# A two-layer hybrid encoder (pooling, RWKV-7, SwiGLU): where ScalarE scales the running state in chunks 4 to 7 of each head pair

## The reference, cut to what matters

```python
kk = heads(k * k_k)
kk = kk / jnp.maximum(jnp.sqrt(jnp.sum(kk * kk, axis=-1, keepdims=True)), 1e-12)
k = k * (1 + (a - 1) * k_a)
...
def wkv_step(S, inp):
    r_t, w_t, k_t, v_t, a_t, b_t = inp
    sa = jnp.einsum('bhvk,bhk->bhv', S, a_t)
    S = S * w_t[:, :, None, :] + sa[..., None] * b_t[:, :, None, :] + v_t[..., None] * k_t[:, :, None, :]
    y = jnp.einsum('bhvk,bhk->bhv', S, r_t)
    return S, y
```

## Time and profile before

| | us |
|---|---|
| three runs | 2701.8, 2696.0, 2696.34 |
| median | 2696.34 |
| the profiled execution, its own time | 2696.08 |
| its span, first to last instruction | 2694.3 |

### The profile page before, as it was taken

How to read it: one execution, slowest core, us unless ns; L and a number is a source line. 1 busy time by engine, 2 the same in 40 slices (tenths; PEclk the granted TensorE clock), 3 DMA queues, 4 the chain that set the end, 5 groups by cost and what they waited for, 6 DMA issues and landing times. The chain is left out here.

```text
span 2694.3 us, 65806 instructions
## 1 busy us (share of the span) xinstructions
PE 2547.0 (95%) x27280; PEld 2455.0 (91%) x27280; DVE 1685.1 (63%) x2492; ACT 932.5 (35%) x1942; POOL 1586.1 (59%) x1303
## 2 busy tenths in 40 slices
PE   8999999978888999999999999998888899999997
PEld 8999999967777999999999999988777789999996
DVE  6876328656654789931598971576555548899124
ACT  3444013444531345410245530244354214454002
POOL 6556665734324677666767766666334257776665
PEclk9999999999998999999999999999999979999998
DMA  4222232100001232223322222321000112322332
GB/s 152 95 103 85 87 99 79 63 3 5 4 20 34 86 102 99 89 87 94 93 96 95 102 82 86 100 74 41 4 4 5 35 41 94 102 95 84 88 91 77
DMA packets 81898, 193.65 MB, mean 72 GB/s; under 512 B 13680, under 2 KB 14064, under 8 KB 81648
## 3 DMA queue, kind: packets, MB, share of 16 engines
q1 hardware_dynamic: 78192, 187.07, 21.5%
q10 hardware_dynamic: 3456, 3.02, 0.4%
HBM read 186.95 MB, written 3.12 MB: 71 GB/s over the span
## 5 line engine op out<-in xcount | busy, mean ns | idle before, releaser
L850 PE MATMUL ps<-xa,w_hi 128*128 128x272 f32 x2208 | 583.3, 289 | 4.0 <-DVE w_lo L1744 2.4
L850 PE MATMUL ps<-xa,w_lo 128*128 128x272 f32 x1932 | 560.6, 290 | 0.0
L642 POOL TENSOR_SCALAR w_hi<-w_raw 128x1024 fp32r<-128x1024 f32 (+2 forms) x225 | 244.2, 1085 | 405.3 <-PE ps L736 397.5
L850 PE MATMUL ps<-xb,w_hi 128*128 128x272 f32 x1656 | 478.8, 289 | 0.0
L850 PEld LDWEIGHTS ps<-xa,w_hi 128*128 128x128 f32 x2208 | 399.1, 189 | 6.1 <-DVE w_lo L1744 2.8
L646 POOL TENSOR_TENSOR w_lo<-w_raw,w_hi 128x640 fp32r<-128x640 f32 (+2 forms) x225 | 365.5, 1624 | 0.0
L850 PEld LDWEIGHTS ps<-xa,w_lo 128*128 128x128 f32 x1932 | 364.2, 189 | 0.0
L850 PEld LDWEIGHTS ps<-xb,w_hi 128*128 128x128 f32 x1656 | 312.7, 189 | 0.0
L736 PE MATMUL ps<-hh,w_hi 128*128 128x272 f32 x1472 | 305.0, 288 | 5.6 <-DVE hl L1772 5.4
L736 PE MATMUL ps<-hh,w_lo 128*128 128x272 f32 x1472 | 302.7, 288 | 0.0
L736 PE MATMUL ps<-hl,w_hi 128*128 128x272 f32 x1472 | 302.3, 287 | 0.0
(11 more groups left out here) (351 smaller groups left out, 5667.4 us busy)
## 6 DMA issues: line engine op xcount, KB each, us to landing
w_raw<-in_wz SPq DMA_DIRECT2D x44, 512.0 KB, 3.2
w_odd<-in_w1i SPq DMA_DIRECT2D x72, 256.0 KB, 2.9
w_odd<-in_w2i SPq DMA_DIRECT2D x72, 256.0 KB, 2.9
w_raw<-in_w1i SPq DMA_DIRECT2D x68, 256.0 KB, 2.8
w_raw<-in_w2i SPq DMA_DIRECT2D x64, 256.0 KB, 2.8
w_raw<-in_w1o SPq DMA_DIRECT2D x32, 448.0 KB, 3.3
w_raw<-in_w2o SPq DMA_DIRECT2D x32, 448.0 KB, 3.3
w_raw<-in_w2i SPq DMA_DIRECT2D x20, 512.0 KB, 3.2
```

The lines of the kernel that those rows point to most:

```text
L642: pool.tensor_scalar(w_hi[k][:, 0:nk, :], w_raw[k][:, 0:nk, :], 1.0, 0.0, ALU.mult, ALU.add).then_inc(w_hi_done, 1)
L850: mm = pe.matmul(ps[:, bank(site, b, j), 0:HT], w, x, start=(j in FRESH and k + i == 0), stop=(k == 3 and i == 2), skip_group_check=True)
```

## The change

ScalarE's list alone is changed. In every `half_a` with `right`, carry(c) moves from slot c + 1 to slot c, for c = 4 to 7: carry(4) stands in slot 4 right behind the OUT copies. `sample_state` moves from slot 4 to slot 6, behind carry(6) and ahead of y_tile(2). Where a next pair is prepared too (`nxt and right`, four `half_a` a layer), a new dictionary moves piece 5 (the table load and the root) from slot 4 to slot 5, behind carry(5), and the rate scaling from piece 3 in slot 3 to a piece 4 in slot 4, behind carry(4). The two calls a layer with `right` but no `nxt` have only the moves of carry and `sample_state`.

```diff
+        IN_A_ACT = {1: (1,), 2: (2,), 3: (3,), 4: (4,), 5: (5,)}
...
+                if k == (3 if p < 2 else 4):
+                    act.wait_ge(scan_ready, n + 1)
                     act.wait_ge(sig_ready, n * 4 + 4)
                     act.activation(tB[:, :], aa[:, :], ACT.Identity, scale=col(l, p + COL["k_a"]), bias=col(l, p + COL["one_ka"])).then_inc(kf_ready, 1)
...
-                    if right and k == 4:
+                    if right and 4 <= k < 8:
+                        carry(k, l, p - 1)
+                    if right and k == 6:
                         sample_state(l, p - 1)
-                    if right and 5 <= k < 9:
-                        carry(k - 1, l, p - 1)
...
-                    for q in IN_A.get(k, ()) if nxt else ():
+                    for q in IN_A_ACT.get(k, ()) if nxt and right else IN_A.get(k, ()) if nxt else ():
                         prepare_1(l, p + 1, q, not right)
```

## The result

The changed kernel takes 2718.2 us (median of 5 runs, 2713.1 to 2724.5); the kernel before takes 2696.0 on the same chips. The ratio is 1.0081, with a 95% interval of 1.0065 to 1.0098. The forecast had the direction, and the start times within a pair to about 0.05, but 10.5 us where 22 were lost; 2718 lies outside its range. The profiled execution of after took 2718.2, with a span of 2716.4, so span against span it is 22.1 more.

A forecast was written before the change was run, and what follows sets the result against it. TensorE was busy 95% of the span, so ScalarE counted only where others wait for it. 6 x 1.55 + 2 x 0.33 + 2 x 0.29 + 2 x 0 = 10.5 us more gave 2706.8 us, range 2699 to 2715.

The forecast's parts named there:

- Part 1: carry(4) in slot 4: VectorE no longer waits for it, S of chunk 4 starts 0.59 us earlier.
- Part 2: Rate scaling in slot 4: no effect, since ScalarE would wait there for S of chunk 4 anyway.
- Part 3: ScalarE's root behind carry(5): it starts 2.33 us late, at 2073.16 against 2070.83.
- Rival (d): ScalarE must be emptied at the table switch in the new place, 1.28 us more before the root: 2717; chance 0.02.
- Part 4: sample_state and y_tile(2): TensorE newly waits, state_y of chunk 6 comes 0.38 us later, S of chunk 6 0.30 late.
- Part 5: GpSimd's Newton step to VectorE's L2003: slack 0.78 us, so L2003 and half_b come 1.55 late; L2003's length stays 1.06.
- The slack of two low-clock pairs: Two of the eight half_a, with TensorE's clock low, have more slack before L2003: 0.33 us late each.
- Rival (c): TensorE waits at L856 and its clock falls to 1.2 GHz in six more half_a, 7.3 us more: 2714; chance 0.12.
- (a): The table load runs ahead of carry(5)'s wait, so the root is only 0.90 us late: 2698; chance 0.06.
- (b): Only the carry chain counts, L2003's delay being taken up behind L856: 2699.3, chance 0.10; with y_tile(2) in time 2691.6, chance 0.05.
- (e): The change has no effect, its order unchanged in effect or voided by the slots' waits: 2696; chance 0.02.

The follow-up runs named there:

- Experiment 6: Kernel before with carry(4) to carry(7) one slot earlier and sample_state in slot 7, root and rate scaling unmoved: 2680.1 us, ratio 0.9942.
- Experiment 3: Changed kernel with GpSimd's two rows y x rsz moved from behind kkb to the start of half_a: 2703.8 us, ratio to before 1.0027.
- experiment 2: Kernel before with the root alone moved, to slot 6 behind carry(5) and ahead of y_tile(2): 2719.6 us, ratio 1.0084.
- experiment 1: Changed kernel with root and rate scaling put back where they were, carries and sample_state still moved: 2692.6 us, ratio to before 0.9976.
- experiment 4: Changed kernel with two extra 272-column matmuls on TensorE ahead of the head sum's wait, for p > 1: 2712.0 us, ratio to before 1.0054.
- experiment 5: Kernel before with GpSimd's two rows y x rsz moved to the start of half_a: 2693.3 us, ratio 1.0001.
- experiment 7: Kernel before with the edits of experiment 5 and Experiment 6 together: 2680.4 us, ratio 0.9950.
- experiment 8: experiment 7 plus five 272-column matmuls, one in each of slots 0 to 4 of each layer's final half_a: 2678.9 us, ratio to before 0.9932.

## Why the forecast had the mechanism and half the size

**Part 1** (0.59 earlier) was right: S stands 0.61 after tq. Experiment 6 shows that even alone it brings only 0.14 a pair at the end.

**Part 2** (rate scaling, nothing) was right: it runs at 650.64, and carry(5) behind it waits 1.38 for S all the same.

**Part 3** (root 2.33 late) was right: load 0.36 after the carry, root 1.30 after the load. Rival (d) named 2717, near the result, but by a drain that is not there; in after too the root follows the load by 0.02, so the 1.28 is all that a load costs here, and the 2.66 of the Trainium skill (ScalarE: Activation LUTs, What ACT_TABLE_LOAD costs) is not seen. That the two numbers meet is chance.

**Part 4** (0.38 later at `state_y`, S of chunk 6 0.30 late) was right within 0.04: 1.84 from S to L965 against 1.88, 2.52 from S to S against 2.51.

**Part 5 failed, in one sentence:** "I take L2003's 1.06 as unchanged, since GpSimd's L672 starts with it again", with 1.14 as the upper bound. The start was right (7.08 after the root, forecast 7.09), and the wait nearly so, 1.14 (forecast about 1.3). But the rows and the product had not started together before. In before GpSimd's rows start 0.86 ahead of the product; in after both are released by kkb's end, and the rows start 0.08 ahead. The product then lies beside the first row for nearly its whole length. It took 1.84: 8 x 0.78 = 6.2 us that the sum lacks. The forecast read three lengths, 0.78, 1.06 and 1.14, and took 1.06 for the price of an overlap and 1.14 for its bound, where each was the price of a part of one. Experiment 3 shows this by taking the rows away: the root is as late, the wait for kkb is the same, and the product takes 0.78.

**The slack of two low-clock pairs** (2 x 0.33 in place of 2 x 1.55) was wrong as a mechanism: in after all eight pairs wait 1.14 for kkb, and the falls that made the slack are gone from their places. In time it was no error by itself. The 0.33 is 1.55 less the 1.22 that such a fall had cost in before, and with the fall gone those 1.22 come back. What the sum lacks is the price of the falls of after, about 8.5 us in the pairs. Against that, before has a third fall in its pairs (at 1960 us), which leaves L2003 at 7.87 behind the root and which the forecast did not count; its 1.5 are gone too.

**Rival (c), the clock,** had 0.12 and happened on top of the forecast, in five of eight. It was set against a wait of 1.3 us; the wait is 1.99, as the product is longer, and experiment 3 shows no fall behind a wait of 0.94. So the two errors are for a good part one chain: late root, product beside the rows, long wait, clock. Whether a wait of 1.3 would have kept the clock up, no run shows. Rivals (a), (b) and (e) are excluded by the rows above, and by experiment 2.

**The sum, set right,** without the falls of either kernel: 8 x (1.55 + 0.78) = 18.6, 2 x 0.3 = 0.6, together 19.2. The table above has 22.8 + 3.35 - 3.1 - 1.0 = 22.1; what lies between is +4.2 in the four pairs and +2.75 in the last pairs, where the clock fell more often than in before (eight times against three), -3.1 in the final `half_a`, where it stood at 1.2 GHz for less long (mean 0.82 over 821 to 868 us, against 0.78 over 808 to 855 in before), and -1.0 elsewhere, which was not traced further.

## What to carry to other kernels

When an operation is delayed until its releaser also releases work on another engine, ask how long it takes beside that work from its first nanosecond: read its length against its offset in all places of the trace, not its mean. A step that is late by more than its slack can cost more than the lateness, since the wait that it opens on TensorE can take the clock with it (how much of the 22 us that was in the median is not settled). Of a change with several moves, try each alone: here the carries alone gained 0.6% (most of it by the clock, whose part in it is not explained), and the root's late place alone cost 0.8%.

## What the runs showed of the hardware

**VectorE's product is held up while one of GpSimd's rows runs, and the trace shows the hold as the product's own length.** All of these are the same 128x544 operation, and each is the offset of its start from the rows' start and its length:

| kernel | rows started before it by | length | end after rows' start |
|---|---|---|---|
| before | 0.86 | 1.06 | 1.92 |
| experiment 1 | 0.72 | 1.20 | 1.92 |
| experiment 6 | 0.39 | 1.53 | 1.92 |
| experiment 4, two pairs | 0.33 and 0.28 | 1.60 and 1.64 | 1.93 and 1.92 |
| after | 0.08 | 1.84 | 1.92 |
| before, the two pairs with a fall ahead of the product | 2.08 and 2.11 | 1.14 and 1.10 | 3.22 and 3.21 |
| experiments 3, 5, 7, 8 | no rows | 0.78 | |

Beside the first row it ends 1.92 after the rows' start wherever it begins, and the rows pay too: 3.11 for two in place of 2.63. The last line but one is the product of the earlier trace rows and its like in layer 1. Here is GpSimd beside that of the earlier trace rows:

```profile
748.96 2.63 POOL L672 TENSOR_TENSOR y<-y,rsz 128x544 f32<-128x544 f32 x2
```

That product begins beside the second row, which ends at 751.59, and ends 0.58 to 0.59 behind it; no row stands behind to pay for it. A first row of 1.34 gives the same: 1.92 - 1.34 = 0.58. So in every line the product ends about 0.58 after the end of the row beside which it began. The Trainium skill (SBUF — State Buffer, Terms) has VectorE and GpSimd share a pair of ports that is held for the whole instruction, so that the loser stands still; and (GPSIMD Engine Reference, 1. Specifications) that a VectorE instruction with two SBUF inputs, as this one with zs and tB, is among those that contend. The trace agrees in kind: the end goes with the row's end and not with the product's start. In size it has 0.2 less: a row alone takes 1.34, and standing still until then would make 1.34 - 0.08 + 0.78 = 2.04 in after and 1.26 in before, against 1.84 and 1.06.

**TensorE's clock.** After a wait of 1.99 at the head sum it fell to 1.2 GHz in five of eight, after one of 2.6 in five of eight too (experiment 2), and after 0.94 to 0.98 in none of thirteen (experiments 3 and 4); four of after's five cost 1.1 to 1.2 us each, one 2.4. With those waits shortened, falls stood at other places of the pairs, where after has none. The long stretch in the final `half_a` costs 6.5 to 8 us a layer (44.6 to 46.2 against 38.1 between the last two head sums). It is there or not in kernels whose code is alike at that place, and even between the two layers of one execution (experiments 2, 6 and 7). The times of one kernel go roughly with the mean clock of the run: experiment 1 took 2679.4 at 0.990 and 2697.6 at 0.982. The long stretch is as large as the gain of a good edit, and what sets it is open.
